# Block seams of a two-block transformer: fillers, gates, a narrow projection and weight splits moved

## The reference

```python
def first_block(x, mem, ...):                      # two layers
    h = h + 0.5 * swiglu_ffn(rms_norm(h, ffn1_norm[l]), ffn1_w_in[l], ffn1_w_out[l])
    h = h + hybrid_mixer(rms_norm(h, mix_norm[l]), w_in[l], ...)
    h = h + memory_cross_attention(rms_norm(h, xattn_norm[l]), rms_norm(mem, mem_norm[l]), ...)
    h = h + 0.5 * swiglu_ffn(rms_norm(h, ffn2_norm[l]), ffn2_w_in[l], ffn2_w_out[l])

# in hybrid_mixer
proj = xn @ w_in                                   # sb_qkv, gdn_qkv, gdn_z, gdn_a, gdn_b (4 + 4 columns: "ab")
z = jnp.einsum('bhtd,bhsd->bhts', qb, kb) * scale  # stick-breaking attention, 8 heads of 64
log_beta = jax.nn.log_sigmoid(z)
log_1m_beta = jnp.where(causal, log_beta - z, 0.0)
between = lax.cumsum(log_1m_beta, axis=3, reverse=True) - log_1m_beta
a = jnp.where(causal, jnp.exp(log_beta + between), 0.0)
# gated delta rule (GDN), 4 heads of 128, chunks of 64
lower = jnp.where(strict, jnp.einsum('bhnck,bhnek->bhnce', kbeta, k) * decay, 0.0)
sol = lax.linalg.triangular_solve(lower + eye, rhs, left_side=True, lower=True)
return jnp.concatenate([sb, go], axis=-1) @ w_out

# second_block: FFN, attention of three kinds (24 maps) with gates, FFN; two layers
branches = jnp.einsum('bsnw,nwd->bsnd', ys, w_branch[l])
gates = jax.nn.sigmoid(gate_logits.reshape(b, s, N_BRANCH, D_MODEL))
merged = jnp.sum(gates * branches, axis=2)
x = x + merged @ w_out[l]
```

## Time and profile before

| what | us |
|---|---|
| median of 3 timed runs (2796.66 to 2802.59) | 2796.67 |
| profiled execution | 2789.85 |
| its span | 2788.0 |
| TensorE busy in it (96%) | 2689.6 |
| VectorE busy (55%) | 1529.0 |
| ScalarE busy (50%) | 1383.2 |
| GpSimd busy (9%) | 239.2 |

### The profile page before, as it was taken

How to read it: one execution, slowest core, us unless ns; L and a number is a source line. 1 busy time by engine, 2 the same in 40 slices (tenths; PEclk the granted TensorE clock), 3 DMA queues, 4 the chain that set the end, 5 groups by cost and what they waited for, 6 DMA issues and landing times.

```text
span 2788.0 us, 39499 instructions
## 1 busy us (share of the span) xinstructions
PE 2689.6 (96%) x14976; PEld 2304.6 (83%) x14976; DVE 1529.0 (55%) x2109; ACT 1383.2 (50%) x2167; POOL 239.2 (9%) x147
## 2 busy tenths in 40 slices
PE   8999998999999999899999999999999999999998
PEld 6889887888888898787888889778888888888887
DVE  5566624455555664455556546456555555556554
ACT  5456335454544552445445445455545444456543
POOL 0100201000000002100010000442000000243000
PEclk9999999999999999999999999999999999999999
DMA  6554212355555441144755554224555554323553
GB/s 246 187 177 158 83 46 98 121 177 185 196 188 183 158 143 47 61 144 132 219 186 182 183 188 155 96 99 151 189 182 183 186 188 159 121 91 125 193 188 136
DMA packets 117803, 427.54 MB, mean 153 GB/s; under 512 B 13004, under 2 KB 14796, under 8 KB 117132
## 3 DMA queue, kind: packets, MB, share of 16 engines
q1 hardware_dynamic: 117152, 424.59, 45.0%
q10 hardware_dynamic: 492, 0.69, 0.1%
HBM read 423.79 MB, written 1.44 MB: 153 GB/s over the span
## 4 chain that ended last, share of the span: by engine, by line
PE 87%; DVE 7%; ACT 4%; issue 2%; DMA 0%; POOL 0%; ACTq 0%; DVEq 0%; SPq 0%
PE bank L454 72%; DVE lo_slots L442 2%; PE bank L1545 2%; PE bank L474 2%; ACT hi_slots L428 1%; PE bank L646 1%; PE bank L1592 1%; PE bank L1561 1%; PE bank L952 1%; PE bank L1109 1%; PE bank L593 1%; PE bank L1120 1%; DVE x_lo L625 1%; PE bank L839 0%; ACT junk L561 0%
## 5 line engine op out<-in xcount | busy, mean ns | idle before, releaser
L442 DVE TENSOR_TENSOR lo_slots<-raw,hi_slots 128x1024 fp32r<-128x1024 f32 x740 | 914.2, 1240 | 789.9 <-ACT hi_slots L428 789.9
L428 ACT ACTIVATE hi_slots<-raw 128x1024 fp32r<-128x1024 f32 x788 | 830.4, 1057 | 667.2 <-PE bank L454 647.0
L454 PE MATMUL bank<-hi_slots,x_hi 128*128 128x512 f32 x1600 | 635.5, 397 | 13.0 <-DVE x_lo L625 7.7
L454 PE MATMUL bank<-hi_slots,x_lo 128*128 128x512 f32 x1600 | 626.4, 391 | 0.0
L454 PE MATMUL bank<-lo_slots,x_hi 128*128 128x512 f32 x1600 | 625.3, 391 | 0.0
L454 PEld LDWEIGHTS bank<-hi_slots,x_hi 128*128 128x128 f32 x1600 | 302.1, 189 | 75.9 <-issue 11.7
L454 PEld LDWEIGHTS bank<-hi_slots,x_lo 128*128 128x128 f32 x1600 | 301.4, 188 | 63.6
L454 PEld LDWEIGHTS bank<-lo_slots,x_hi 128*128 128x128 f32 x1600 | 302.3, 189 | 59.6
L454 PE MATMUL bank<-x_hi,hi_slots 128*128 128x256 f32 x1152 | 335.8, 291 | 6.1 <-DVE lo_slots L442 4.2
L454 PE MATMUL bank<-x_lo,hi_slots 128*128 128x256 f32 x1152 | 328.9, 286 | 0.0
L454 PE MATMUL bank<-x_hi,lo_slots 128*128 128x256 f32 x1152 | 328.5, 285 | 0.0
(11 more groups left out here) (314 smaller groups left out, 3134.9 us busy)
## 6 DMA issues: line engine op xcount, KB each, us to landing
raw<-w_full SPq DMA_DIRECT2D x792, 512.0 KB, 3.3
bias_mem<-bias_rows SPq DMA_DIRECT2D x8, 288.0 KB, 5.8
mem<-mem_t SPq DMA_DIRECT2D x2, 1024.0 KB, 8.0
const<-consts SPq DMA_DIRECT2D x1, 1664.0 KB, 6.9
h<-x_t SPq DMA_DIRECT2D x1, 1024.0 KB, 5.3
final<-finals SPq DMA_DIRECT2D x2, 512.0 KB, 7.2
out_t<-h SPq DMA_DIRECT2D x4, 256.0 KB, 2.3
bias_rows<-junk ACTq DMA_DIRECT2D x1, 384.0 KB
```

What stands on the lines that cost most here:

```text
L428: nc.scalar.activation(w_hi[s], raw[s][:, :], ACT.Copy).then_inc(hi_ready[s], 1)
L442: nc.vector.tensor_tensor(w_lo[s], raw[s][:, :], w_hi[s].bitcast(F32), ALU.subtract).then_inc(lo_ready[s], 1)
L454: mm = nc.tensor.matmul(out, lhsT=a, rhs=b, start=start and n == 0, stop=stop and n == len(passes) - 1)
```

## The change

The program still computes the same with the same units of weights, in another order and with some steps in another form.

- **ab**: the 8 weight columns become the stationary side and the 256 tokens the moving one: 24 matmuls in place of 48. The result has 8 rows; DVE copies them out and TensorE turns them with two transposes behind group 4.
- **GDN**: both token tiles' keys and values are turned first, into their own banks; then, per tile, beta rows, the value pair and the dots. `lower` is multiplied by decay and beta first and by the dots last. Weight splits of group 6 stand elsewhere on DVE and ACT.
- **Stick**: value units at steps 0, 1, 8 and 9, none at 2 to 7; the output projection's units 0, 1 and 2 stand before AV of the last head, before the head sums, and before the spread. Four value units (before: two) stand around the turning.
- **Hand-over**: the last two weight splits stand behind the turning on ACT and on DVE.
- **Block 1**: three gates before attention (two before); gates are evicted as tanh of half the value, and `dve_gated` uses (tanh + 1) times the branch, halved when the merged sum is split; branch units 0 to 4 stand at steps 21 to 25 (before: 0 and 1 at 23 and 24); the head norm stands amid the next units, with tiles of its own; POOL splits the first four branch units' successors.

Constants:

```diff
-MEM_OPEN, MEM_KEPT = 2, 2
+MEM_OPEN, MEM_KEPT = 2, 4
+MEM_EVACS = KT + KT // 2
+VALUE_BANKS = (2, 3, 1, 3)
...
-STICK_ACCS, STICK_TURNS = ((0, 1), (2, 3)), ((4, 5), (6, 7))
+STICK_ACCS, STICK_TURNS = ((0, 5), (2, 3)), ((4, 5), (6, 7))
...
-MERGE_ORDER = (2, 3, 0, 1)
-STICK_VALUES = (2, 3, 5, 6, 8, 9)
+BRANCH_BANKS = (2, 3, 2, 3, 2, 3, 0, 1, 0, 1, 0, 1)
+STICK_VALUES = (0, 1, 8, 9)
 SB_ORDER = (2, 3, 0, 1)
+GDN_TURNS, GDN_ROWS = ((6, 7), (0, 1)), (5, 3)
 GATES = N_BRANCH * KT
-ROPE_GATES = 2
+ROPE_GATES = 3
```

ab, GDN on TensorE, and DVE's part on `lower`:

```diff
-                           [(x_hi[:, k, cut], x_lo[:, k, cut], ab_now_hi[:, k * 8:k * 8 + 8],
-                             ab_now_lo[:, k * 8:k * 8 + 8]) for k in range(KT)])
-            mm.then_inc(sems["ab_ps"], 1)
+            three(bank[4][0:8, 0:TOK], [(ab_now_hi[:, k * 8:k * 8 + 8], ab_now_lo[:, k * 8:k * 8 + 8], x_hi[:, k, :],
+                                         x_lo[:, k, :]) for k in range(KT)]).then_inc(sems["ab_ps"], 1)
             pe_section(E, 1, 1, 3, x_hi, x_lo)
...
+            for t in range(TT):
+                mm = nc.tensor.transpose(bank[4][:, 8 * t:8 * t + 8], ab_rows[:, t * P:(t + 1) * P], c("ident", 0, 8)[0:8, :])
+            mm.then_inc(sems["ab_tp"], 1)
...
                 if t:
-                    pe.wait_ge(sems["decay_pre"], E.after("decay_pre", t))
-                    pe.wait_ge(sems["eg"], E.after("eg", t))
-                for hd in range(GDN_HEADS):
-                    mm = nc.tensor.matmul(bank[5][:, hd * P:(hd + 1) * P],
-                                          lhsT=gate[:, G_LOG, 4 * t + hd:4 * t + hd + 1].broadcast_to([P, P]),
-                                          rhs=c("chunk_cum"), start=True, stop=True)
-                mm.then_inc(sems["row_ps"], 1)
-                pe_token_pair(E, 6, 6, 2, x_hi, x_lo, (t,))
+                    pe.wait_ge(bank_free[GDN_ROWS[t]], E.evac(6))
+                pe_gate_rows(G_LOG, t, bank[GDN_ROWS[t]], c("chunk_cum")).then_inc(sems["row_ps"], 1)
+            pe.wait_ge(sems["decay_act"], E.after("decay_act", 6))
+            pe.wait_ge(sems["decay_dve"], E.after("decay_dve", 6))
+            for t in range(TT):
+                cut = slice(t * P, (t + 1) * P)
+                if t:
+                    pe.wait_ge(sems["lower"], E.after("lower", 1))
+                pe_gate_rows(G_BETA, t, bank[4], c("ident")).then_inc(sems["row_ps"], 1)
+                pe_token_pair(E, 6, 6, 2, x_hi, x_lo, (t,), [bank[2][:, tile_cut(n)] for n in range(TT)])
                 pe.wait_ge(sems["kv_scaled"], E.after("kv_scaled", 3 * t + 3))
-                for hd in range(GDN_HEADS):
-                    mm = nc.tensor.matmul(bank[7][:, hd * P:(hd + 1) * P], lhsT=gdn[:, 4 + hd, cut], rhs=gdn[:, hd, cut],
-                                          start=True, stop=True)
-                mm.then_inc(sems["row_ps"], 1)
-                for hd in range(GDN_HEADS):
-                    mm = nc.tensor.matmul(bank[6][:, hd * P:(hd + 1) * P], lhsT=gdn[:, 4 + hd, cut],
-                                          rhs=gdn[:, 4 + hd, cut], start=True, stop=True)
-                mm.then_inc(sems["row_ps"], 1)
-                for hd in range(GDN_HEADS):
-                    mm = nc.tensor.matmul(bank[4][:, hd * P:(hd + 1) * P],
-                                          lhsT=gate[:, G_BETA, 4 * t + hd:4 * t + hd + 1].broadcast_to([P, P]),
-                                          rhs=c("ident"), start=True, stop=True)
-                mm.then_inc(sems["row_ps"], 1)
+                for b, first in zip(GDN_TURNS[t], (4, 0)):
+                    for hd in range(GDN_HEADS):
+                        mm = nc.tensor.matmul(bank[b][:, hd * P:(hd + 1) * P], lhsT=gdn[:, 4 + hd, cut],
+                                              rhs=gdn[:, first + hd, cut], start=True, stop=True)
+                    mm.then_inc(sems["row_ps"], 1)
...
+                cut = slice(t * P, (t + 1) * P)
+                keys, queries = (bank[b] for b in GDN_TURNS[t])
+                dve.wait_ge(sems["row_ps"], E.after("row_ps", 3 * t + 3))
+                dve.wait_ge(sems["decay"], E.after("decay", t + 1))
+                nc.vector.tensor_tensor(lower[:, t, :], decay[:, t, :], bank[4][:, :], ALU.mult).then_inc(sems["lower"], 1)
+                if t == 0:
+                    split_lo(E, E.mid(6, 0))
+                dve.wait_ge(sems["row_ps"], E.after("row_ps", 3 * t + 4))
+                dve.wait_ge(sems["lower"], E.after("lower", 2 * t + 1))
+                nc.vector.tensor_tensor(lower[:, t, :], lower[:, t, :], keys[:, :], ALU.mult).then_inc(sems["lower"], 1)
+                dve.wait_ge(sems["row_ps"], E.after("row_ps", 3 * t + 5))
                 dve.wait_ge(sems["eg"], E.after("eg", t + 1))
                 nc.vector.tensor_tensor(gdn[:, 0:4, cut], gdn[:, 0:4, cut], heads(exp_g[:, t, :]),
                                         ALU.mult).then_inc(sems["qdec"], 1)
-                dve.wait_ge(sems["decay"], E.after("decay", t + 1))
-                nc.vector.tensor_tensor(qk_decay[:, t, :], decay[:, t, :], bank[7][:, :], ALU.mult).then_inc(sems["qkd"], 1)
-                dve.wait_ge(sems["row_ps"], E.after("row_ps", 4 * t + 4))
-                nc.vector.tensor_tensor(lower[:, t, :], decay[:, t, :], bank[6][:, :], ALU.mult).then_inc(sems["lower"], 1)
...
-                        split_lo(E, E.mid(6, 2 * lev + t))
+                if lev in (2, 3):
+                    split_lo(E, E.mid(6, lev))
             for n in range(3):
```

Stick and the seam:

```diff
+        def pe_stick_out(E, j):
+
+            def opened(i, hf):
+                if j == 0:
+                    pe.wait_ge(sems["hn_lo"], E.after("hn_lo", 2))
+                    pe.wait_ge(sems["sbo"], E.after("sbo", 3))
+                    pe.wait_ge(sems["lm"], E.after("lm", SB_HEADS))
+                if j == 1:
+                    pe.wait_ge(sems["mem_ev"], E.after("mem_ev", KT + 2))
+                if i >= 2 and hf == 0:
+                    pe.wait_ge(sems["hn_lo"], E.after("hn_lo", i + 1))
+
...
+                if i == SB_HEADS + 2:
+                    pe_stick_out(E, 0)
...
             pe_head_spread(E, 1, SB_DIM)
+            for j in range(3, KT):
+                pe_stick_out(E, j)
 
         def act_stick(E):
...
+                if i == 4:
+                    act_mem_next(E, KT + 1)
+                if i == SB_HEADS + 1:
+                    act_mem_next(E, KT + 3)
+            act.wait_ge(sems["sbo"], E.after("sbo", 4))
+            act_head_squares(E, 1, sbo)
             act.preload_act_table_set("sqrt_and_others")
-            act.wait_ge(sems["sbo"], E.after("sbo", 4))
-            act_head_norm(E, 1, sbo, SB_DIM)
-            act.wait_ge(sems["hn_gate"], E.after("hn_gate", 1))
-            act_head_parts(E, 0, go, x_hi[:, 4:8, :])
-            act.wait_ge(sems["hn_gain"], E.after("hn_gain", 8))
-            act_head_parts(E, 1, sbo, x_hi[:, 0:4, :])
+            act_head_root(E, 1, SB_DIM)
+            for j in range(4):
+                if j >= 2:
+                    act.wait_ge(sems["hn_gain"], E.after("hn_gain", 2 * j + 2))
+                    act_head_part(E, 1, sbo, x_hi[:, 0:4, :], j - 2)
...
-                            pe.wait_ge(sems["hn_lo"], E.after("hn_lo", 2 if i < 2 else 4))
-
-                        pe_residual(E, 2, 11, SB_ORDER, STICK_ACCS, opened, nothing)
-                        pe.wait_ge(sems["h_ready"], E.state(2) * PARTS + 2)
-                        pe_mem_values(E, KT // 2 - 1, 0)
+                        for t in range(TT):
+                            pe_mem_values(E, 2, t)
                         pe_turn_scaled(E, 1, STICK_TURNS)
-                        pe_mem_values(E, KT // 2 - 1, 1)
-                        pe.wait_ge(sems["mem_ev"], E.after("mem_ev", MEM_UNITS))
+                        for t in range(TT):
+                            pe_mem_values(E, 3, t)
```

Hand-over on DVE (on ACT alike):

```diff
                 split_lo(E, u0 + i)
             for t in range(TT):
                 dve_sum(E, st, 0, t, accs, 1.0, u0 + KT - 2)
-            split_lo(E, u0 + KT - 2)
             dve_sum(E, st, 1, 0, accs, 1.0, u0 + KT - 1)
-            dve_turned(normed, 0, turns, gain)
+            dve_turned(normed, 0, turns, gain, (0, 2))
             dve_sum(E, st, 1, 1, accs, 1.0, u0 + KT - 1)
-            split_lo(E, u0 + KT - 1)
+            dve_turned(normed, 0, turns, gain, (2, 4))
```

Block 1:

```diff
+        def branches_at(E, step):
+
+            m = ROPE_GATES + step - GATES
+            return [m] if E.block == 1 and m >= 0 else []
+
...
-            nc.scalar.activation(sig[:, g, :], bank[2 + g % 2][:, 0:TOK], ACT.Copy).then_inc(bank_free[g % SLOTS], 1)
+            nc.scalar.activation(sig[:, g, :], bank[2 + g % 2][:, 0:TOK], ACT.Tanh, scale=0.5).then_inc(bank_free[g % SLOTS], 1)
...
-                if E.block == 1 and len(maps) - 1 <= i <= len(maps):
-                    pe_branch_unit(E, 0, i - len(maps) + 1)
+                for m in branches_at(E, i):
+                    pe_branch_unit(E, m)
...
+
+            n, s = divmod(m, SLOTS)
```

(11 more changed lines are left out.)

395 lines of the change are left out of this document (215 added, 180 removed).

## The result

The changed kernel takes 2723.12 us (median of 4 runs, 2719.41 to 2723.83), the kernel before 2798.29 (4 runs, 2796.66 to 2802.59): a ratio of 0.9726, 95% interval 0.971 to 0.9743, that is 75 us or 2.7% faster. The forecast was 2738, range 2717 to 2760. The profiled execution took 2723.83 us with a span of 2721.8, 66.2 less than the span before.

The account below looks back on a forecast made before the run. TensorE bounds the kernel (busy 2689.6 of 2788.0 us). Savings 9 + 10 + 18 + 7 + 3.2 + 11 = 58 us gave 2732 profiled and, 6.8 us being the profiled-to-timed difference, 2738 timed; range 2717 to 2760.

Parts of the forecast that it names:

- rival 3: Whole kernel: more gain than granted, stick 12 us a layer, GDN and tail whole, 10 us more: 2728; chance 0.17.
- "right": Signs: log_rest, norm-square, cross-projection lo-split and FFN x_lo waits gone; AV waits 1 to 3 us, steps 3 to 7; probs under 1.5.
- "wrong": Signs: half-clock stick steps, new lo-split waits, small DVE instructions stretched beside POOL splits, 1.2 GHz still following the ab matmuls.
- ab: Projection in both layers: fewer matmuls and no clock drop save 9 us; 4 to 6 if the clock still falls.
- work term: In the ab projection: 24 matmuls of 2.8 us plus transposes save 3.55 and 2.25 us in the two layers.
- clock term: At the ab projection: 1.6 us more saved in each layer if TensorE no longer falls to 1.2 GHz.
- GDN: Both layers: waits for `lower` and level masks shrink, less 1.2 us a layer kept back; 10 us saved, between 4 and 12.
- Stick and seam: Stick attention to cross projection: 17 us available less 9 new idle, taken as 9 a layer, 18; bounds 6 and 24.
- rival 1: Clock takes back much in stick steps and ab: 14 us less gain, 2752; 0.23 for this or the POOL/waits rival alone.
- Hand-overs: Four hand-overs to an FFN: splits moved behind the turning shorten x_lo waits by 1.75 us each, 7 in all.
- Block 1: Two layers: third early gate saves 3.2 us, units covering the attention's end and merged-sum waits save 11.
- Rival 2: Waits move: POOL splits hold DVE up, tail and GDN gain half, 10 us less, 2748; 0.23 for this or rival 1 alone.

## Why the prediction was right, and where it was not

The measured 2723.12 us lies inside the range, but below my forecast's own 2730 to 2746 (0.45), in the band of rival 3 (2717 to 2729, 0.17). Rival 3's reasons were more from the stick steps, GDN and the attention's end. What the stretches show in excess is in block 1, and 9 us more lie in the step from the profiled to the timed run. Of the signs named, those of "right" came in the main (AV's waits in steps 3 to 5 alone), and two of "wrong" with them: half-clock stretches in the stick steps, and DVE's small instructions stretched beside POOL splits.

**ab.** Forecast 9; alone 7.2 between single profiles. The work term is right: the ab matmuls take 2.8 us each time. The clock term was half right: behind the ab matmuls the drop is gone in every profile with the new form, but in layer 0 others came later.

**GDN.** "ab to z" saved 20.0 in all, 19 were forecast for both terms. That close a fit is partly luck in the pair of profiles: three of the old form have 355.2 to 362.0 us over both layers, nine of the new 332.0 to 338.2, which makes 23 between the means. The waits shown in the earlier trace rows for L1074 and L1109, 9.7, are now 3.7 (L1124 for L1351), where 2.4 were kept back. The reasons are only partly tested: the late splits' place is worth nothing, so one cause that the prediction named, the splits standing behind levels 2 and 3, is out. What is left are the turnings ahead, the products' order, and the other splits leaving the levels. Which of these gives what stays open.

**Stick and seam.** Saved 22.4 with two hand-overs, forecast 21.5 (between the means of three profiles and five it is 26). The places were right: the new idle time stands at AV, 1.8, 0.8 and 3.0 us in steps 3 to 5 of layer 0, log_rest's wait is gone, and with ACT's new order and the output units that of the squares. The size of the new idle time was not: 5.6 us in that layer for the 9 that the circle of the earlier trace rows gave, none of it listed in steps 6 and 7. The drop of the clock in the bare steps, which the 9 a layer left out, came for 13.7 us in layer 0 and 6.8 in layer 1. That is a part of rival 1; it cost less than the 10 us of its 14 that it took from the stick. A likely reason, not tested by itself: in steps bound by the circle TensorE at 1.2 GHz fills what would be idle time (13.65 busy of 13.70 in the row at 415.90). The two runs with ACT's work and the value units moved put the whole of it, waits and clock, at 3 to 4 us a layer.

**Hand-overs.** Forecast 7; alone the waits fell by 7.8 and the span by 6.2, in the changed kernel the waits by 8.4: right in mechanism and size, with the clock's part unsettled.

**Block 1.** This term was mis-sized: 14.2 forecast; 24.3 measured with the hand-overs, 20.8 when the 3.5 forecast for these is taken off. The step that failed is that the sum counted one half-clock stretch there, at 1878.4. The kernel before has four more between the rotation and FFN 2 (stretches, columns as in the earlier trace rows), the first two behind the wait for the turned queries, the third at the end of layer 1's attention, the fourth at its hand-over:

```profile
1748.70:1752.10 3.40, 3.40 (x14) 0.50 0.62 195
2397.30:2400.70 3.40, 3.40 (x16) 0.50 0.66 220
2526.95:2530.35 3.40, 2.81 (x13) 0.50 0.16 61
2591.80:2595.20 3.40, 3.40 (x10) 0.50 0.31 113
```

The changed kernel has none in these stretches. Added up from each matmul's start to the next one's, layer 0's gate units take 3.0 us less than before, for a wait of 1.6, and the branch units' 7.1 us less, where I had 5.5. The longest wait kept back, 1.3 us, was right to a tenth. How the clock's part divides between the gates, the attention's end and the hand-over stays open: the one at 2591.8 and half of that at 1878.4 also went with the hand-over alone, and the one at 1748.7 is missing in runs that keep the wait ahead of it (ab alone). And that the units at steps 21 to 25 cover the wait is read off the waits; no run takes them away by themselves.

**Rival 2** had its sign wrong: the POOL splits do stretch DVE's small instructions, by 0.7 us, and with them on DVE the long wait is back.

**From the profiled to the timed run.** I carried 6.8 us from the one to the other. That step failed, in the kernel's favour: the changed kernel's profiled run (2723.83) is one of its four timed ones, the longest. The kernel before took 2789.9 to 2791.5 in 7 runs on one chip, with a mean granted clock of 0.984 to 0.985, 0.984 as in its profile, and 2801.6 and 2802.0 in one run each on two others, with 0.980; whether the chip sets this is not shown. Beside its profile the changed kernel gains 66 us, beside the timed runs 75. The forecast of 58 is 8 short of the first and 17 of the second.

## What to carry over

Read the stretches at the lower clock as part of each wait that precedes them, and count them with it: those that I left out are likely most of what block 1 gave beyond the forecast. A filler between dependent steps is worth its length only as far as the chain of the other engines is not renewed by the same step: put the fillers' evictions and splits where an engine waits in its circle, not behind the instruction that closes it. And a slow split on an engine that nobody waits for is cheaper than a fast one in the queue that everybody waits for.

## What the runs showed of the hardware

- Equal instructions took 165.96 to 169.31 us over one stretch with only the drops to 1.2 GHz different (6.8 us of it at that clock in the shortest, 13.7 in the longest); a single profile can't settle 3 us there.
- In the stick steps TensorE fell to 1.2 GHz after 13.4 us with 10.58 us busy, and in the run with value units at steps 5 and 8 for 8 and 9 it stayed at 2.4 GHz for 6.5 us longer than in the changed kernel, with the sum of the waits nearly unchanged (10.1 for 10.6).
- 88 more table loads of 1.28 us, 113 us on ACT, made block 1 longer by 21 us; the load ahead of the exp ran before the exp's wait for DVE.
